# Bias and key choice of a sparse softmax: added by VectorE, or accumulated by matmuls

## What is computed

```
sc  = where(key_pos <= t_pos, indexer_scores, -inf)
idx = top_k(sc, 64);  valid = idx <= t_pos
logits = q . k[idx] * Dh ** -0.5                      # 8 heads, 2 groups of 4 share a key head
bias   = rel_bias[rel_bucket(t_pos - idx)]            # per head
logits = where(valid, logits + bias, -1e30)
p = softmax(logits);  o = p @ v[idx]
```

## Time and profile before

| | before |
|---|---|
| time, median of 3 | 1466.6 us (1459.32 to 1467.17) |
| the profiled execution | 1467.17 us, its span 1465.5 us |
| TensorE busy | 1441.3 us |
| VectorE busy | 842.6 us |
| ScalarE busy | 584.8 us |
| GpSimd busy | 112.7 us |
| mean granted clock of TensorE | 0.988 |

### The profile page before, as it was taken

One profiled execution on the slowest core, in us unless ns is written; L12 is line 12 of the kernel. 1 busy time (PEld: TensorE's weight loads), 2 busy tenths in 40 slices (PEclk: granted clock), 3 DMA queues, 4 the chain that ended last, 5 costly groups with the idle time before them and its releaser, 6 DMA issues.

```text
span 1465.5 us, 28712 instructions
## 1 busy us (share of the span) xinstructions
PE 1441.3 (98%) x10698; PEld 1412.6 (96%) x10698; DVE 842.6 (57%) x1165; ACT 584.8 (40%) x702; POOL 112.7 (8%) x160
## 2 busy tenths in 40 slices
PE   7999999999999999999999999999999999999998
PEld 6988989889899999999999999999999999999998
DVE  6555865655577655555555444555555556666654
ACT  6335742463633433333333333333333333334432
POOL 2003022211022100000000000000000001111000
PEclk9999998999899999999999999999999999999999
DMA  7657453334355455445544555555545445556553
GB/s 280 199 132 223 156 173 125 101 117 130 135 193 164 151 172 167 163 161 168 165 163 143 167 164 170 183 169 161 162 166 165 161 134 160 170 167 205 162 161 113
DMA packets 72547, 238.92 MB, mean 163 GB/s; under 512 B 9392, under 2 KB 10512, under 8 KB 72120
## 3 DMA queue, kind: packets, MB, share of 16 engines
q1 hardware_dynamic: 67184, 224.54, 47.7%
q0 software_dynamic: 3536, 11.46, 2.4%
q10 hardware_dynamic: 1784, 2.32, 1.0%
HBM read 232.43 MB, written 5.86 MB: 163 GB/s over the span
## 4 chain that ended last, share of the span: by engine, by line
PE 93%; DMA 2%; issue 2%; DVE 1%; ACT 1%; POOL 0%; SPq 0%; ACTq 0%; DVEq 0%; POOLq 0%
PE acc L405 29%; PE acc L407 29%; PE acc L406 29%; DMA w_raw<-in_w_in 1%; DMA out_gla_s<-proj 1%; PE px L1406 1%; PE px L1469 1%; PE px L1357 1%; PE px L1333 0%; PE px L1376 0%; PE px L1500 0%; PE px L405 0%; PE px L407 0%; PE px L406 0%; DMA proj<-in_xT 0%
## 5 line engine op out<-in xcount | busy, mean ns | idle before, releaser
L374 DVE TENSOR_TENSOR w_lo<-w_raw,w_hi 128x1024 fp32r<-128x1024 f32 (+2 forms) x450 | 513.0, 1144 | 320.4 <-ACT w_hi L368 312.6
L368 ACT ACTIVATE w_hi<-w_raw 128x1024 fp32r<-128x1024 f32 (+2 forms) x450 | 443.5, 989 | 588.7 <-PE acc L407 573.8
L405 PE MATMUL acc<-n_hi,w_hi 128*128 128x288 f32 x1664 | 492.9, 296 | 0.0
L406 PE MATMUL acc<-n_lo,w_hi 128*128 128x288 f32 x1664 | 491.4, 295 | 0.0
L407 PE MATMUL acc<-n_hi,w_lo 128*128 128x288 f32 x1664 | 489.7, 294 | 0.0
L407 PEld LDWEIGHTS acc<-n_hi,w_lo 128*128 128x128 f32 x1664 | 313.8, 189 | 0.0
L406 PEld LDWEIGHTS acc<-n_lo,w_hi 128*128 128x128 f32 x1664 | 312.5, 188 | 0.1
L405 PEld LDWEIGHTS acc<-n_hi,w_hi 128*128 128x128 f32 x1664 | 311.9, 187 | 0.1
L405 PE MATMUL acc<-x_hi,w_hi 128*128 128x288 f32 x928 | 283.0, 305 | 14.7 <-DVE w_lo L856 9.8
L406 PE MATMUL acc<-x_lo,w_hi 128*128 128x288 f32 x928 | 277.1, 299 | 0.0
L407 PE MATMUL acc<-x_hi,w_lo 128*128 128x288 f32 x928 | 276.0, 297 | 0.0
(11 more groups left out here) (246 smaller groups left out, 801.4 us busy)
## 6 DMA issues: line engine op xcount, KB each, us to landing
w_raw<-in_w_gu SPq DMA_DIRECT2D x176, 512.0 KB, 4.0
w_raw<-in_w_in SPq DMA_DIRECT2D x82, 512.0 KB, 4.4
w_raw<-in_w_down SPq DMA_DIRECT2D x64, 384.0 KB, 3.1
w_raw<-in_w_down SPq DMA_DIRECT2D x64, 320.0 KB, 3.0
w_raw<-in_w_ple SPq DMA_DIRECT2D x32, 576.0 KB, 3.8
w_raw<-in_w_out SPq DMA_DIRECT2D x32, 512.0 KB, 4.1
proj<-in_xT SPq DMA_DIRECT2D x4, 576.0 KB, 6.4
proj<-in_cache_k POOLq DMA_DIRECT2D x16, 128.0 KB, 4.3
```

The lines of the kernel that those rows point to most:

```text
L368: nc.scalar.activation(whi[:, slot, 0:kt * P], raw[:, slot, 0:kt * P], ACT.Copy).then_inc(S("w_hi_done"), 1)
L374: nc.vector.tensor_tensor(wlo[:, slot, 0:kt * P], raw[:, slot, 0:kt * P], whi[:, slot, 0:kt * P].bitcast(F32), ALU.subtract).then_inc(S("w ...
L405: nc.tensor.matmul(out, w_h, m_hi_[:, k0 + k, :], start=first and k == 0, stop=False)
L406: nc.tensor.matmul(out, w_h, m_lo_[:, k0 + k, :], start=False, stop=False)
```

## The change

The bias and the choice are no longer added by VectorE. TensorE accumulates them in PSUM ahead of the logits: for each bank a matmul of the identity with the bias, one of a new constant `bigI` (1e30 times the identity) with the choice, and then the logits of the bank's heads on top. `sc` now holds -1 where it held -1e30, and is read for all heads of a bank by a repeated address. VectorE takes the maximum from PSUM, and ScalarE's exponentials read PSUM and write `prob`. The waits for the bias and for `sel_ready` move from VectorE to TensorE; the wait that `prob` is free (`pt_mm`) moves from VectorE to ScalarE. The constants grow by 128 columns.

```diff
-CONST = {"ident": (P, P), "lev": (P, 7 * P), ...
+CONST = {"ident": (P, P), "bigI": (P, P), "lev": (P, 7 * P), ...
+    put("bigI", np.eye(P) * BIG)
 mask_choice (GpSimd):   fill=-BIG  ->  fill=-1.0
 pick (VectorE):         MARK, -BIG, ALU.not_equal, ALU.mult  ->  MARK, -1.0, ALU.not_equal, ALU.mult
@@ scalar, softmax(u)
+                logits = px[:, 2:4, :].rearrange("p b s -> p (b s)")[:, 0:NR * nk].rearrange("p (r s) -> p r s", r=NR)
                 act.wait_ge(S("max_ready"), u + 1)
+                if u:
+                    act.wait_ge(S("pt_mm"), u)
                 for r in range(NR):
-                    one_ = prob[:, r * nk:(r + 1) * nk]
-                    ins = A(one_, one_, ACT.Exp, bias=sm[:, r:r + 1], accum_out=sm[:, 4 + r:5 + r])
+                    ins = A(prob[:, r * nk:(r + 1) * nk], logits[:, r, :], ACT.Exp, bias=sm[:, r:r + 1],
+                            accum_out=sm[:, 4 + r:5 + r])
@@ vector, softmax(u)
-                dve.wait_ge(S("bias_loaded"), 48)
-                dve.wait_ge(S("sel_ready"), tt + 1)
-                if u:
-                    dve.wait_ge(S("pt_mm"), u)
-                link(V.tensor_tensor(pr, bias_p[:, NR * g:NR * g + NR, SEQ - nk:SEQ],
-                                     sc[:, tt, 0:nk].unsqueeze(1).broadcast_to([P, NR, nk]), ALU.add))
                 dve.wait_ge(S("lg_ready"), u + 1)
-                link(V.tensor_tensor(pr, logits, pr, ALU.add))
-                V.tensor_reduce(sm[:, 0:4], pr, AX.X, ALU.max, negate=True).then_inc(S("max_ready"), 1)
+                V.tensor_reduce(sm[:, 0:4], logits, AX.X, ALU.max, negate=True).then_inc(S("max_ready"), 1)
@@ tensor, softmax(u)
                 if u == 0:
                     pe.wait_ge(S("sc_s_read"), 1)
+                    pe.wait_ge(S("bias_loaded"), 48)
                 else:
                     pe.wait_ge(S("mix_out"), u)
+                pe.wait_ge(S("sel_ready"), tt + 1)
                 pe.wait_ge(S("norm_done"), 5)
                 for r0 in range(0, NR, per):
                     bank = px[:, 2 + r0 * nk // 512, :]
+                    M(bank, ident, bias_p[:, NR * g + r0:NR * g + r0 + per, SEQ - nk:SEQ], start=True, stop=False)
+                    M(bank, C["bigI"], sc[:, tt, 0:nk].unsqueeze(1).broadcast_to([P, per, nk]), start=False, stop=False)
                     for r in range(per):
                         ins = M(bank[:, r * nk:(r + 1) * nk], proj[:, NR * g + r0 + r, P * tt:P * tt + P],
-                                proj[:, ROW_K + g, 0:nk], start=True, stop=True)
+                                proj[:, ROW_K + g, 0:nk], start=False, stop=r == per - 1)
```

More of the change, by code:

```diff
@@ L101 @@
 }
-CONST = {"ident": (P, P), "lev": (P, 7 * P), "tril": (P, P), "wsm": (TS, TS),
+CONST = {"ident": (P, P), "bigI": (P, P), "lev": (P, 7 * P), "tril": (P, P), "wsm": (TS, TS),
          "scan": (P, T), "e16": (IH, 64), "wbm": (64, NB * TS), "adm": (TS, TS), "admneg": (TS, TS),
@@ L499, in mask_choice @@
                 pool.wait_ge(S("picked"), tt + 1)
-                nc.gpsimd.affine_select(out=diag[tt], in_=diag[tt], compare_op=ALU.is_ge, fill=-BIG, base=0,
+                nc.gpsimd.affine_select(out=diag[tt], in_=diag[tt], compare_op=ALU.is_ge, fill=-1.0, base=0,
                                         pattern=[[-1, P]], channel_multiplier=1).then_inc(S("sel_ready"), 1)
@@ L959, in pick @@
                 if r1 == KSEL_P // 8:
-                    V.tensor_scalar(sc[:, tt, 0:nk], sc[:, tt, 0:nk], MARK, -BIG, ALU.not_equal, ALU.mult)\
+                    V.tensor_scalar(sc[:, tt, 0:nk], sc[:, tt, 0:nk], MARK, -1.0, ALU.not_equal, ALU.mult)\
                         .then_inc(S("picked"), 1)
@@ L987, in softmax @@
             def softmax(u):
-                tt, g, nk = u // 2, u % 2, P * (u // 2 + 1)
+                nk = P * (u // 2 + 1)
                 logits = px[:, 2:4, :].rearrange("p b s -> p (b s)")[:, 0:NR * nk].rearrange("p (r s) -> p r s", r=NR)
-                pr = prob[:, 0:NR * nk].rearrange("p (r s) -> p r s", r=NR)
-                dve.wait_ge(S("bias_loaded"), 48)
-                dve.wait_ge(S("sel_ready"), tt + 1)
-                if u:
-                    dve.wait_ge(S("pt_mm"), u)
-                link(V.tensor_tensor(pr, bias_p[:, NR * g:NR * g + NR, SEQ - nk:SEQ],
-                                     sc[:, tt, 0:nk].unsqueeze(1).broadcast_to([P, NR, nk]), ALU.add))
                 dve.wait_ge(S("lg_ready"), u + 1)
-                link(V.tensor_tensor(pr, logits, pr, ALU.add))
-                V.tensor_reduce(sm[:, 0:4], pr, AX.X, ALU.max, negate=True).then_inc(S("max_ready"), 1)
+                V.tensor_reduce(sm[:, 0:4], logits, AX.X, ALU.max, negate=True).then_inc(S("max_ready"), 1)
                 dve.wait_ge(S("exp_ready"), u + 1)
                 link(V.reciprocal(sm[:, 8:12], sm[:, 4:8]))
+                pr = prob[:, 0:NR * nk].rearrange("p (r s) -> p r s", r=NR)
                 V.tensor_tensor(pr, pr, sm[:, 8:12].unsqueeze(2).broadcast_to([P, NR, nk]), ALU.mult)\
```

## The result

The changed kernel takes 1471.22 us (median of 13 runs, 1468.76 to 1477.16) against 1464.78 (13 runs, 1457.97 to 1469.33): ratio 1.0053, 95% interval 1.0036 to 1.0070, or +7.8 us (5.3 to 10.2); the two medians lie 6.4 us apart, the two means 8.4. The forecast was +9.0. One execution of the kernel before, at 1987 us with a mean granted clock of 0.653, is left out everywhere. The profiled execution has a span of 1470.1 us, 4.6 us more than before.

What follows compares the result with a forecast made beforehand. TensorE, busy 1441.3 of 1465.5 us, was taken to bound the kernel: 10.3 - 1.5 + 0.2 = +9.0 us on 1466.6 gives 1475.6 us, 0.6% slower. Its own range was 1473 to 1478 us, the wide one 1467 to 1484.

Steps and rivals of the forecast that it cites:

- the twelve matmuls: TensorE, four softmax steps: 2 + 2 + 4 + 4 f32 matmuls of 512 moving columns add 10.3 us.
- 0.86 us each, from `mix`: Price of each wide matmul on TensorE, taken from the instruction pair of `mix`, which has the same form.
- The upper bound: Price from the logits of step 3: 0.97 us for 512 columns, 11.6 us for twelve matmuls.
- The lower bound: Price from the fp32r matmuls of a tile group: 0.24 us for 512 columns, 2.8 us for twelve.
- The 1.5 us given back: Step 3: the transposes on TensorE no longer wait for L1002, VectorE's last softmax operation, which saves 1.5 us.
- Low clock neutral: Wide matmuls of steps 1 and 2 run doubled at 1.2 GHz but push tile matmuls out, so full-clock price.
- The rival that a stretch shrinks: A low-clock stretch falls away or shrinks, saving about 5 us: net +4, 1470.6 us; chance 0.13.
- The 0.2 us for tile matmuls pushed out of the stretches: Tile matmuls gain a factor of 1.8, not 2, from the high clock, costing about 0.2 us in all.
- The waits moved to TensorE: Waits for `sel_ready` and the bias ahead of the logits cost nothing, with 9.9 and 8.6 us of cover.
- PSUM read in place of SBUF: VectorE's maximum (L999) and ScalarE's exponentials read PSUM instead of SBUF; priced at nothing.
- The removed 7.6 us of VectorE: VectorE loses L995 and L998 in each softmax step: 2 x 1.38 + 2 x 2.44 = 7.6 us of its time.
- the wide one: Range of 1467 to 1484 us, reaching to one low-clock stretch more or less and the scatter between runs.

Runs made afterwards that it cites:

- the kernel that keeps VectorE's adding: Kernel before with the 12 wide matmuls added ahead of the logits, which overwrite them; VectorE still adds bias and choice: ratio 1.0047.
- no wide matmuls: Changed kernel without its 12 wide matmuls; neither TensorE nor VectorE adds bias and choice, which are left out of the result: ratio 0.9982 to before.
- the version with the bias early: Kernel before with VectorE adding bias and choice of step 3 one slot earlier, in slot 30: ratio 0.9978.
- the halves: Kernel before with one of two edits: bias and choice of step 3 one slot earlier (ratio 0.9978), or logits of step 1 in PSUM bank 3 (0.9979).
- steps 1 and 2: Kernel before with 6 wide matmuls, overwritten by the logits, in softmax steps 1 and 2 only: ratio 1.0035.
- steps 0 and 3: Kernel before with 6 wide matmuls, overwritten by the logits, in softmax steps 0 and 3 only: ratio 1.0017.

## Why the prediction was right, step by step

- **TensorE bounds, and the twelve matmuls are charged in full: right.** 10.3 us forecast, 10.7 and 10.1 measured by taking them away and doubling them.
- **0.86 us each, from `mix`, not 0.97 or 0.24: right.** The upper bound had the step's entry of 0.2 us in it, which moved and wasn't paid again. The lower bound is real for one pass of fp32r, 0.23 us. By the Trainium skill ("TensorE: Matmul & The Clock Gate", Back-to-back issue gap), the sustained rate of 131 ns for 512 columns, taken four times for each f32 matmul as in the prediction, would give an estimated 6.3 us for twelve. The rows don't agree with it; they agree with the 216 ns of the formula that the page gives for a single matmul: four times 0.216 is 0.86.
- **The 1.5 us given back: right in the profile, with the reason half told.** The prediction argued both that TensorE comes later and that VectorE's chain gets shorter. Each alone does it: the first in the kernel that keeps VectorE's adding, the second in the one with no wide matmuls.
- **Low clock neutral, each matmul charged at full clock: right on average.** Doubled rows in steps 1 and 2, and yet no double price. The profiled execution had shorter stretches than that of before and ended only 4.6 us later; over all runs the time at 0.50 didn't differ measurably. The rival that a stretch shrinks did describe the profiled execution; as an effect of the change it isn't shown, and the version with the bias early had shorter stretches still with no edit ahead of them. The 0.2 us for tile matmuls pushed out of the stretches is too small for any run here to show.
- **The waits moved to TensorE: right, nothing.** No wait for GpSimd.
- **PSUM read in place of SBUF: right, nothing.** The maximum over 1024 columns takes 1225 ns from PSUM and took 1220 from SBUF, and ScalarE's busy time stays (584.5 us against 584.8).
- **The removed 7.6 us of VectorE:** 6.7 measured, worth nothing to the time.
- **Sum:** +9.0 forecast, +7.8 measured (5.3 to 10.2), +7.5 ± 0.3 at equal clock. The time itself, 1471.2 us, lies below the forecast's own range of 1473 to 1478 us and inside the wide one. The forecast of 1475.6 was 4.4 us too high; 1.8 of that is its starting point, a median of three runs (1466.6), where thirteen give 1464.8.
- **The 1.5 us between the sum and +7.5.** The edits seem to give back more than the waits that they remove: 3.2 ± 0.4 us with no wide matmuls and no adding, where the wait is 1.5; 2.3 for 1.2 and 1.9 for 0.7 with the halves. But the stretch itself has no such microsecond. The kernel before takes 88.76 us (88.75 in its second profile) from the transposes of step 0 to those of step 3 (the earlier trace rows show the end, 292.62; the start is below), 4.85 more than the kernel with no wide matmuls. The wait is 1.5 of it, and 6.8 us less at half clock are about 3.4:

```profile
203.86 0.44 PE px L1369 x4
```

From there to the end, with 13.6 us at 0.50 in each, the profiles of before take 1172.9 and 1172.2 us, those of the changed kernel and of the one with no wide matmuls 1172.0 and 1172.1. The likelier place is the zero of the comparison. The kernel before, run again, lies 0.9 ± 0.4 us below its other 95 runs. Measured from these 12 runs, each with an error of about 0.5 us, the changed kernel is at +8.3 (sum of the terms 8.8), no wide matmuls at -2.4 (-1.5), steps 1 and 2 at +5.1 (5.2), steps 0 and 3 at +3.7 (3.7), the halves at -1.5 (-1.2) and -1.1 (-0.7). Differences between two experiments, such as the 10.7 and 10.1 us for twelve wide matmuls, don't hang on this zero. Twelve runs don't prove it, and why a kernel's own runs should lie lower than those taken beside it stays open. TensorE's wait for the load of `h` at about 400 us, which changed from profile to profile (0 to 1.8 us), is 0.2 us or none in the profiles of before, of the changed kernel and of the one with no wide matmuls, so it doesn't explain the difference between those.

## What to carry to other kernels

Where TensorE is busy for 98% of the span, an addition on VectorE costs only what TensorE waits for it, here 1.5 us in four softmax steps; moving it into matmuls costs their columns in full, 0.86 us for each 512 in f32. Most of the same 1.5 us, and 0.7 more, were to be had by starting the addition a slot earlier and using a free PSUM bank. If the move is wanted for another reason, operands that are exact in fp32r, as the choice with its 0 and -1, should go in fp32r: 0.23 us in place of 0.86.

## What the runs showed of the hardware

- The scatter of one kernel goes with the low clock: at a mean granted clock of 0.994 the changed kernel's runs average 1469.4 us (7 runs), at 0.990 1473.9 us (3 runs); the kernel before has 1461.4 (15 runs) and 1466.4 (17 runs). In every profile the clock fell twice behind or within the runs of 16-column matmuls, in which TensorE was busy throughout; the stretches at 1.2 GHz there lasted 10.2, 6.8 or 3.4 us from one profile to the other, and in the version with the bias early they were shorter than in the kernel before with nothing changed ahead of them. Most profiles have two more stretches at 1.2 GHz, which start between 355 and 410 us.
- A moving operand with a repeated address (four heads reading the same 128 columns) streams as fast as one without: 0.86 us for 512 columns in f32 both.
